# Mixer and norm order changed, x tiles loaded earlier: a two-pass decoder layer on Trainium2

## The chip, the cores and the metric

The kernel runs on the 8 cores of one Trainium2 chip. Each core does its own share of the tokens; nothing is exchanged between cores. The metric is the device time in microseconds of the slowest core, as the median of several runs. A change of more than 2% counts as faster or slower.

## What is computed

One decoder layer, cut to its core:

```python
h = x + 0.5 * rmsnorm(swiglu(rmsnorm(x, g1), wg1, wu1, wd1), p1)
n = rmsnorm(h, gm)
b_a, c_a, h_a, u, v = split(n @ w_in)
y_a = b_a * causal_dwconv3(c_a * h_a)
y_b = u * (tril(w_s[head]) @ rmsnorm(v) + b_s[head])
h = h + rmsnorm(concat(rmsnorm(y_a), rmsnorm(y_b)) @ w_out, pm)
h = h + 0.5 * rmsnorm(swiglu(rmsnorm(h, g2), wg2, wu2, wd2), p2)
h = h + rmsnorm(sigmoid(h @ w_pg) * (p @ w_pp), pp)
```

The model width is 1024, the hidden width 2816, and each core has 2048 prompt tokens (one sequence) and 128 sample tokens (16 sequences of 8).

## The kernel before

A core works its 17 blocks of 128 tokens in two passes: pass 0 has 9 blocks (8 of the prompt, 1 of samples) in three column tiles of 384, pass 1 has 8 blocks in two tiles of 512. Each pass goes through the same stages: gate and up products of the first FFN (`gu_stage`), its down product (`tok_stage`), the mixer, the output projection (`tok_stage`), the second FFN, and the per-layer embedding (`ple`). PE is busy nearly all the time.

Weights come in 44 "fills" a pass. A fill is two DMAs issued by POOL (L259, cast from f32 to bf16) into one of 8 slots of a ring. Before fill f, POOL waits until its slot is released by PE and fill f-3 has landed (`MAXFLY`, L255). `release` issues the next fill, or, where `hold_fills` has set a limit, notes it as owed; `pay_owed` raises the limit and issues what is owed. These limits act while the program is written: what reaches the chip is the order of POOL's instructions and the waits that stand before them.

The first norm works on the transposed input. `xt_load` (L361, on SP's queue) brings an x tile, `x_square` (L465) squares it on ACT, `x_stat` (L477) sums over the channels with 8 matmuls against a matrix of ones and forms 1/rms on ACT, and `x_apply` (L489) writes the 8 normed pieces to nT on DVE. Each following matmul of the tile waits for its own piece only. At the start SP issues x tile 0, and tiles 1 and 2 once fills 0 and 1 (their first halves) have landed; 90 matmuls on ones keep PE busy meanwhile. The units of a `gu_stage` have hooks that put the next tile's norm between them.

The mixer works tile by tile: v products, the norm of the tile before (`norm_tile`, L735: statistic of y_b on PE, then 8 multiplies on DVE), b products (DVE multiplies them in, ACT squares them into one of 4 buffers `sq`), the spatial mix on PE (L784), the statistic of y_a (L799, 4 matmuls in `stat`, L692), and the u products. The last tile's norm is the hook `tail`, behind the first block of the output projection.

`ple` goes over groups of three blocks: gate products into three PSUM pairs (L538), a sigmoid of each on ACT, the embedding product (L853) into the pair that the sigmoid has freed, the product of the two on DVE, the norm, the sum, and the store of y (L872, SP's queue). The result buffers `gb(b)` are six, so the sigmoid of block b waits for the store of block b-6 (`gb_guard`), and the first products of pass 1 write over buffers whose stores must have landed (`guard1`, L911). In pass 0, `ple` also starts the next pass: it loads both x tiles of pass 1 once the last transposed block has landed, squares tile 0 behind group 1, and does its statistic and its multiplies in group 2.

## Time and profile before

| | |
|---|---|
| median of 3 runs | 1377.72 us (1377.32 to 1531.78) |
| the profiled execution | 1379.56 us |
| its span, slowest core (7) | 1378.5 us |
| PE busy in the span | 1305.4 us (95%) |
| DVE, ACT busy | 524.1 us (38%), 415.0 us (30%) |

All times inside the execution are read from core 7, from the start of its span. "[idle before <-releaser]" at the end of a row is how long the engine had stood still before it, and what ended that.

### The profile page before, as it was taken

The numbers are of one execution on the slowest core, as the hardware profiler recorded it, in microseconds if no ns is written. First come the engines' busy times: TensorE is split into PE (matmuls) and PEld (weight loads), VectorE is DVE, ScalarE is ACT, GpSimd is POOL, SyncE is SP. The second block draws the span as 40 slices with busy tenths as digits, with TensorE's granted clock in tenths as the row PEclk, the third lists the DMA queues.
The fourth block names the chain that finished last, engine by engine and source line by source line (L and its number), as shares of the span: only waits on it lengthen the run. The fifth ranks groups of instructions, "written<-read, shape, count | busy, mean of one in ns | idle before, by whom it ended". The sixth has DMA issues, their size and how long they took to land.

```text
span 1378.5 us, 18493 instructions; the slowest of 8 cores (1363.9 to 1378.5 us)
## 1 busy us (share of the span) xinstructions
PE 1305.4 (95%) x6710; PEld 647.0 (47%) x6710; DVE 524.1 (38%) x691; ACT 415.0 (30%) x860; POOL 94.3 (7%) x185
## 2 busy tenths in 40 slices
PE   5999999999989999999996999999999899999995
PEld 3566664455445666644441444444444344444442
DVE  2322223356677222213365322223466922221337
ACT  3311112344355111111175111123333721111136
POOL 2100000001000200000010000000010020000000
PEclk8999999999999999999997999999999999999998
DMA  9997422129525963231289974321295297423123
GB/s 215 178 222 154 68 47 46 31 45 183 92 42 82 175 124 62 47 69 25 45 202 211 220 159 87 63 53 31 62 175 107 50 147 141 91 48 68 31 39 122
DMA packets 88185, 139.87 MB, mean 101 GB/s; under 512 B 58272, under 2 KB 58528, under 8 KB 87456
## 3 DMA queue, kind: packets, MB, share of 16 engines
q0 software_dynamic: 25296, 90.25, 39.7%
q1 hardware_dynamic: 62800, 48.43, 13.2%
q8 instruction: 56, 0.92, 0.3%
q14 instruction: 33, 0.27, 0.1%
HBM read 206.03 MB, written 9.51 MB: 156 GB/s over the span
## 4 chain that ended last, share of the span: by engine, by line
PE 84%; DVE 6%; DMA 3%; issue 3%; ACT 3%; POOL 0%; DVEq 0%; ACTq 0%; POOLq 0%; SPq 0%
PE ps L218 56%; PE ps L538 23%; PE ps L527 3%; DMA y<-big 2%; DVE zsc L227 2%; DVE nT L227 1%; DVE big L231 1%; DMA h<-xT 1%; ACT big L223 1%; DVE big L227 1%; DMA ring<-w 1%; ACT nT L223 1%; ACT sg L223 1%; ACT L223 1%; DVE nbr L227 1%
## 5 line engine op out<-in xcount | busy, mean ns | idle before, releaser
L218 PE MATMUL ps<-nT,ring 128*128 128x384 bf16 (+1 forms) x4160 | 785.3, 351 | 18.7 <-DVE nT L227 9.2
L218 PEld LDWEIGHTS ps<-nT,ring 128*128 128x128 bf16 x4160 | 409.7, 99 | 392.3 <-issue 44.0
L231 DVE TENSOR_TENSOR big<-ps,sg 128x384 bf16<-128x384 f32 (+1 forms) x220 | 133.9, 610 | 489.4 <-PE ps L218 479.4
L538 PE MATMUL ps<-ring,big 128*128 128x512 bf16 x1320 | 285.5, 379 | 4.5 <-DVE big L231 4.5
L223 ACT ACTIVATE sg<-ps 128x384 f32<-128x384 f32 (+1 forms) x237 | 127.1, 537 | 506.4 <-PE ps L218 496.8
L538 PEld LDWEIGHTS ps<-ring,big 128*128 128x128 bf16 x1320 | 128.9, 98 | 161.0 <-issue 6.2
L259 POOL DMA_DIRECT2D ring<-w x170 | 89.9, 535 | 1104.5 <-PE ps L218 621.6
L223 ACT ACTIVATE big<-ps 128x1024 bf16<-128x1024 f32 (+4 forms) x88 | 75.4, 870 | 229.4 <-PE ps L538 192.4
L227 DVE SCALAR_TENSOR_TENSOR zsc<-ps,st,gains 128x1024 f32<-128x1024 f32 x51 | 65.4, 1282 | 192.5 <-ACT st L223 192.2
L538 PE MATMUL ps<-ring,nT 128*128 128x512 bf16 x480 | 105.4, 379 | 1.0 <-DVE big L231 1.0
L231 DVE TENSOR_TENSOR big<-ps,big 128x384 f32<-128x384 f32 (+3 forms) x77 | 50.8, 686 | 62.1 <-PE ps L218 34.4
L538 PEld LDWEIGHTS ps<-ring,nT 128*128 128x128 bf16 x480 | 46.6, 98 | 58.3 <-issue 3.0
L231 DVE TENSOR_TENSOR h<-h,zsc 128x1024 f32<-128x1024 f32 x51 | 62.5, 1225 | 5.3
L227 DVE SCALAR_TENSOR_TENSOR nbr<-h,st,gains 128x1024 bf16<-128x1024 f32 x34 | 43.6, 1282 | 36.6 <-ACT st L223 36.6
L223 ACT ACTIVATE nbr<-h 128x1024 bf16<-128x1024 f32 x34 | 35.9, 1057 | 59.6 <-DVE h L231 51.7
L223 ACT ACTIVATE st<-st 128x1 f32<-128x1 f32 x204 | 41.4, 203 | 18.5 <-ACT st L223 0.5
L223 ACT ACT_TABLE_LOAD x27 | 34.6, 1283 | 22.0 <-PE ps L218 9.0
L527 PE MATMUL ps<-ring,big 128*128 128x512 bf16 x176 | 38.6, 379 | 0.0
L223 ACT ACTIVATE big<-big 128x384 bf16<-128x384 f32 (+1 forms) x40 | 21.9, 566 | 44.1 <-DVE big L231 44.1
L218 PE MATMUL ps<-ring,nT 128*128 128x512 bf16 x136 | 30.2, 379 | 0.0
L853 PE MATMUL ps<-ring,big 128*128 128x512 bf16 x68 | 18.7, 421 | 9.2 <-ACT big L223 9.2
L527 PEld LDWEIGHTS ps<-ring,big 128*128 128x128 bf16 x176 | 17.2, 98 | 20.8
(63 smaller groups left out, 369.3 us busy)
## 6 DMA issues: line engine op xcount, KB each, us to landing
ring<-w POOLq DMA_DIRECT2D x170, 512.0 KB, 14.5
h<-x SPq DMA_DIRECT2D x17, 512.0 KB, 30.7
y<-big SPq DMA_DIRECT2D x13, 512.0 KB, 10.7
gains<-gain SPq DMA_DIRECT2D x12, 512.0 KB, 9.3
h<-xT SPq DMA_DIRECT2D x3, 1536.0 KB, 13.2
big<-xT SPq DMA_DIRECT2D x2, 2048.0 KB, 20.0
y<-zsc SPq DMA_DIRECT2D x4, 512.0 KB, 12.0
big<-pT POOLq DMA_DIRECT2D x2, 512.0 KB, 7.9
```

Source lines behind the costliest of these rows:

```text
L218: ins = nc.tensor.matmul(out_ap, l, r, start=(i == 0), stop=(i == n - 1))
L223: return ACT.mark(nc.scalar.activation(**kw))
L227: return DVE.mark(nc.vector.scalar_tensor_tensor(out=out, in0=in0, scalar=scalar, in1=in1, op0=op0, op1=op1))
L231: return DVE.mark(nc.vector.tensor_tensor(out=out, in0=in0, in1=in1, op=op))
L259: nc.gpsimd.dma_start(out=ring_t[:, s, o:o + HALF], in_=w_d[f % NFILL, :, o:o + HALF])))
L527: ins = nc.tensor.matmul(o.t, lhs(k), sv[:, k % per, half * 512:half * 512 + 512], start=(k == 0), stop=(k == nk - 1))
L538: ins = nc.tensor.matmul(o.t, lhs(k), sv, start=(k == 0), stop=(k == nk - 1))
L853: ins = nc.tensor.matmul(o.t, pT_v[:, k, b * 128:(b + 1) * 128], sv, start=(k == 0), stop=(k == 1))
```

## The change

At the start, x tile 1 is issued on SP right behind tile 0, tile 2 once POOL has issued two fills; 110 matmuls on ones; both tiles' statistics, then 40 more matmuls on ones, stand before the first product; tile 2 is squared and summed later, in two hooks. In the mixer, `norm_tile` is cut in two: the statistic stays behind the v products, the 8 multiplies go behind the spatial mix; the statistic of y_a goes behind the second u product; `sq` has 6 buffers. In `ple` of pass 0, x tile 0 of pass 1 is issued behind the last down product (hook `next_x`; the junk of `post_stat` is moved out of its place), is squared behind the second sigmoid into a region of its own, summed at the end of the embedding products of group 0, and applied in group 1; x tile 1 is issued behind the stores of group 0; `pay_owed` is called for one fill a group. The norm of tile 1 is cut in two hooks, 32 products later. In the last group of the last pass both embedding products go ahead of the gates, with a fourth pair. The diff, cut:

```diff
+    xt_load(PASSES[0], 1)
...
+    for _ in range(2):
+        issue_next()
     ev_pc = pchain(nc.gpsimd.memset(carry_t[:], 0.0))
+    xt_load(PASSES[0], 2, [ev_pc])
     while wr["issued"] < NSLOT:
         issue_next()
-    for ti in range(1, 3):
-        xt_load(PASSES[0], ti, [fill_ev[ti - 1][0]])
 
     act([ev_ones], out=st_t[:, 0, 0:1], in_=ones_t[:, 0:1], func=AF.Ln)
-    warm = banks[7]
-    PE.wait(ev_ones)
-    for _ in range(90):
-        ins = nc.tensor.matmul(warm.t[:, 0:128], ones_t[:], ones_t[:], start=True, stop=True)
-    warm.free = PE.mark(ins)
+
+    def warm_up(n):
+        PE.wait(ev_ones, banks[7].free)
+        for _ in range(n):
+            ins = nc.tensor.matmul(banks[7].t[:, 0:128], ones_t[:], ones_t[:], start=True, stop=True)
+        banks[7].free = PE.mark(ins)
+
+    warm_up(110)
...
+    def x_sq_at(P, ti):
+        c0, w = P.tiles[ti]
+        if (P.idx, ti) == (1, 0):
+            return bigf[:, 4096:6144].bitcast(BF16).rearrange("p (k s) -> p k s", k=8)
+        return nT_t[:, :, c0:c0 + w]
...
+        sqt = x_sq_at(P, ti)
         X = XT[P.idx, ti].rearrange("p (k s) -> p k s", k=8)
         sq = []
         for i in range(0, 8, 2):
-            o = nT_t[:, i:i + 2, c0:c0 + w]
+            o = sqt[:, i:i + 2, :]
...
-    def x_apply(P, ti, bank, e2):
+    def x_apply(P, ti, bank, e2, wait=None):
         c0, w = P.tiles[ti]
         X = XT[P.idx, ti].rearrange("p (k s) -> p k s", k=8)
         out = []
+        DVE.wait(wait)
...
-                hooks[b]()
+                hooks[b](ev)
...
-        sq = [bigf[:, ZR + 2048 + 256 * i:ZR + 2304 + 256 * i].bitcast(BF16) for i in range(4)]
+        sq = [bigf[:, o:o + 256].bitcast(BF16) for o in [ZR + 2048 + 256 * i for i in range(4)] + [ZR + 4096, ZR + 4352]]
...
-        def norm_tile(ti, bank_of=get_bank):
+        def norm_stat(ti, bank_of=get_bank):
+            c0, w = P.tiles[ti]
+            par = ti % 2
+            return rstd_bc(*stat(y_ev[ti][1], w, bank_of), zsc_t[:, par, 512:1024], w, rs_free[par])
+
+        def norm_apply(ti, e_b):
             c0, w = P.tiles[ti]
             par = ti % 2
             ra, rb = zsc_t[:, par, 0:512], zsc_t[:, par, 512:1024]
-            ya, yb, ev_u = y_ev[ti]
-            e_b = rstd_bc(*stat(yb, w, bank_of), rb, w, rs_free[par])
+            ya, _, ev_u = y_ev[ti]
...
-                norm_tile(ti - 1)
+                e_b = norm_stat(ti - 1)
...
-            e_a = rstd_bc(*stat(sqa, w), zsc_t[:, ti % 2, 0:512], w, rs_free[ti % 2])
+            if ti >= 1:
+                norm_apply(ti - 1, e_b)
             sqb = []
             for c in range(4):
                 b, evl = proj(fU, evU, ti, c)
+                if c == 1:
+                    e_a = rstd_bc(*stat(sqa, w), zsc_t[:, ti % 2, 0:512], w, rs_free[ti % 2])
...
-        def tail():
-            norm_tile(nt - 1, get_tp)
+        def tail(ev):
+            norm_apply(nt - 1, norm_stat(nt - 1, get_tp))
...
-            xt_load(N, 0, [nT_ev[P.nb - 1]])
-            xt_load(N, 1)
-            pay_owed([nT_ev[P.nb - 1]], NFILL + 3)
+            pay_owed([nT_ev[P.nb - 1]], NFILL + 1)
+        def embed(b, last, npair=3):
+            pair = get_pair(npair)
+            pt, lo, hi = pair
+            PE.wait(evp, pT_ev)
+            ins = None
+            for o, half in ((lo, 0), (hi, 1)):
+                for k in range(2):
+                    sv = ring_t[:, fp % NSLOT, k * 1024 + half * 512:k * 1024 + half * 512 + 512]
+                    ins = nc.tensor.matmul(o.t, pT_v[:, k, b * 128:(b + 1) * 128], sv, start=(k == 0), stop=(k == 1))
+            ev = PE.mark(ins)
+            if last:
+                release(fp, ev)
+            return pair, ev
...
+            early = N is None and lastg
+            if early:
+                emb = {b: embed(b, b == grp[-1], 4) for b in grp}
...
-                if N is not None and gi == 2 and b == grp[0]:
-                    xs["st"] = x_stat(N, 0, xs["sq"], get_tp)
...
+                if N is not None and b == 1:
+                    xs["sq"] = x_square(N, 0)
...
-                xs["sq"] = x_square(N, 0, [gate_ev[3]])
+                x_apply(N, 0, *xs["st"], [gate_ev[3]])
...
-            if N is not None and gi == 2:
-                xs["ev"] = x_apply(N, 0, *xs["st"])
+            if N is not None and gi == 0:
+                xs["st"] = x_stat(N, 0, xs["sq"], get_tp)
...
+            if N is not None and not lastg:
+                pay_owed(None, NFILL + 2 + gi)
+                if gi == 0:
+                    xt_load(N, 1, [xstat_ev[1, 0]])
...
-    x_apply(PASSES[0], 0, *x_stat(PASSES[0], 0, x_square(PASSES[0], 0), get_bank))
-
-    def start_mid(ti):
-        def f():
-            x_apply(PASSES[0], ti, *x_stat(PASSES[0], ti, x_square(PASSES[0], ti), get_bank))
-        return f
+    first = x_stat(PASSES[0], 0, x_square(PASSES[0], 0), get_bank)
+    x_apply(PASSES[0], 0, *first)
+    second = x_stat(PASSES[0], 1, x_square(PASSES[0], 1), get_bank)
+    warm_up(40)
+    x_apply(PASSES[0], 1, *second)
+
+    nx = {}
+
+    def start_square():
+        nx["sq"] = x_square(PASSES[0], 2)
+
+    def start_mid():
+        x_apply(PASSES[0], 2, *x_stat(PASSES[0], 2, nx["sq"], get_bank))
...
+    def next_square():
+        nx["sq"] = x_square(PASSES[1], 1)
+
     def next_mid():
-        e = x_apply(PASSES[1], 1, *x_stat(PASSES[1], 1, x_square(PASSES[1], 1), get_bank))
+        e = x_apply(PASSES[1], 1, *x_stat(PASSES[1], 1, nx["sq"], get_bank))
...
-            gu_stage(P, 2, guard1, {(0, 0): (0, start_mid(1)), (1, 0): (1, start_mid(2)), (2, 0): (0, start_loads),
+            gu_stage(P, 2, guard1, {(1, 0): (1, start_square), (1, 1): (0, start_mid), (2, 0): (0, start_loads),
...
-            gu_stage(P, 3, guard1, {(0, 0): (1, next_mid)})
+            gu_stage(P, 3, guard1, {(0, 0): (1, next_square), (1, 0): (1, next_mid)})
...
+        def next_x(ev):
+            xt_load(PASSES[1], 0, [ev])
...
-                  base + G2POST, 4.0, 1, 14, cast)
+                  base + G2POST, 4.0, 1, 0, cast, {8: next_x} if N is not None else None)
```

The order of DVE's instructions in the mixer of pass 0, from the last v multiply of the third tile to its last u multiply. `big<-ps,sv` is a v multiply, `nT<-big,gc,zsc` the multiplies of a tile's norm, `big<-ps,big` the b or u multiplies, `big<-ps,gc,bbc` the mix. Before:

```order
L231 TENSOR_TENSOR big<-ps,sv 128x512 x3
L231 TENSOR_TENSOR big<-big 128x512
L227 SCALAR_TENSOR_TENSOR nT<-big,gc,zsc 128x384 x8
L231 TENSOR_TENSOR big<-ps,big 128x384 x4
L227 SCALAR_TENSOR_TENSOR big<-ps,gc,bbc 128x256
...
L231 TENSOR_TENSOR big<-ps,big 128x384 x4
L227 SCALAR_TENSOR_TENSOR nT<-big,gc,zsc 128x384 x8
```

Now:

```order
L231 TENSOR_TENSOR big<-ps,sv 128x512 x3
L231 TENSOR_TENSOR big<-big 128x512
L231 TENSOR_TENSOR big<-ps,big 128x384 x4
L227 SCALAR_TENSOR_TENSOR big<-ps,gc,bbc 128x256
...
L227 SCALAR_TENSOR_TENSOR nT<-big,gc,zsc 128x384 x8
L231 TENSOR_TENSOR big<-ps,big 128x384 x4
L227 SCALAR_TENSOR_TENSOR nT<-big,gc,zsc 128x384 x8
```

The 8 multiplies of the second tile's norm have moved from ahead of the b multiplies to ahead of the u multiplies.

The order of ACT in `ple` of pass 0, group 0 and the start of group 1. `big<-ps 128x1024` is a sigmoid, `sg,st<-big` the sum of squares of a block, `ps<-ps 128x512 x2` the 1/rms of the x tile. Before:

```order
L223 ACTIVATE big<-ps 128x1024 x3
L223 ACTIVATE sg,st<-big 128x1024
L223 ACTIVATE st<-st 128x1 x2
...
L223 ACTIVATE big<-ps 128x1024
L223 ACTIVATE zsc<-ps 128x1024 x2
L223 ACTIVATE nT<-big 128x2x512 x4
```

Now:

```order
L223 ACTIVATE big<-ps 128x1024 x2
L223 ACTIVATE big<-big 128x1024 x4
L223 ACTIVATE big<-ps 128x1024
L223 ACTIVATE sg,st<-big 128x1024
L223 ACTIVATE st<-st 128x1 x2
...
L223 ACTIVATE ps<-ps 128x512 x2
L223 ACTIVATE big<-ps 128x1024
L223 ACTIVATE zsc<-ps 128x1024 x2
```

The four squares of the x tile stood behind the sigmoids of group 1 and stand now between the second and the third sigmoid of group 0.

The order of SP's queue at the same place. Before:

```order
L325 DMA_TRANSPOSE nT<-nbr 128x8x128 [waits sem_dve,t1]
L293 DMA gains<-gain 128x1024
L361 DMA big<-xT 128x4096 [waits t0]
L361 DMA big<-xT 128x4096
L872 DMA y<-big 128x1024 [waits sem_dve] x4
L872 DMA y<-zsc 128x1024 [waits sem_dve] x2
```

Now:

```order
L361 DMA big<-xT 128x4096 [waits sem_pe]
L325 DMA_TRANSPOSE nT<-nbr 128x8x128 [waits sem_dve,t1]
L293 DMA gains<-gain 128x1024
L901 DMA y<-big 128x1024 [waits sem_dve] x3
L361 DMA big<-xT 128x4096 [waits sem_pe]
L901 DMA y<-big 128x1024 [waits sem_dve]
L901 DMA y<-zsc 128x1024 [waits sem_dve] x2
```

The first x tile has gone ahead of the last transpose, the second behind three stores. POOL's rows for the fills of this place now (t0 is the last transposed block, xt1 the second x tile, slotN_M the landing of a half fill); they are the same, with the same waits, before:

```order
L259 DMA ring<-w 128x2048 [waits t0,sem_pe,slot1_0,slot1_1]
L259 DMA ring<-w 128x2048
L259 DMA ring<-w 128x2048 [waits sem_pe,slot2_0,slot2_1]
L259 DMA ring<-w 128x2048
L259 DMA ring<-w 128x2048 [waits sem_pe,slot3_0]
L259 DMA ring<-w 128x2048
L259 DMA ring<-w 128x2048 [waits xt1,sem_pe,slot4_0,slot4_1]
```

Here nothing has moved.

## Rows read from the trace of the kernel before

**Rows 1.** The cores: span and mean granted clock.

```profile
core 0: 1363.9 us, clock 0.981
core 7: 1378.5 us, clock 0.976
```

**Rows 2.** Two of PE's waits, core 7: us in total, times, longest.

```profile
PE ps L692 <- ACT big L223: 10.3, 11, 3.5
PE ps L853 <- ACT big L223: 9.2, 4, 3.4
```

**Rows 3.** Timeline of the start: start us, us, engine, line, operation, count, idle before.

```profile
1.41 7.52 PE L393 MATMUL ps<-ones 128*128 128x128 bf16 x90 [1.41 <-POOL ones L371]
...
9.96 1.58 ACT L223 ACTIVATE nT<-h 128x768 bf16<-128x768 f32 x2 [7.12 <-DMA h<-xT]
...
27.19 3.04 ACT L223 ACTIVATE nT<-h 128x768 bf16<-128x768 f32 x4 [6.59 <-DMA h<-xT]
28.18 3.00 PE L484 MATMUL ps<-nT,ones 128*128 128x384 bf16 x8 [7.46 <-ACT nT L223]
...
57.40 149.82 PE L218 MATMUL ps<-nT,ring 128*128 128x384 bf16 x921 [0.20 <-DVE nT L227]
```

**Rows 4.** DMA queue of SP, 18 to 26 us: packets, MB, share of 16 engines.

```profile
q1 hardware_dynamic: 133, 1.56, 55.0%
```

**Rows 5.** Timeline of the mixer of pass 0, third tile.

```profile
378.07 4.31 DVE L227 SCALAR_TENSOR_TENSOR nT<-big,gc,zsc 128x384 bf16<-128x384 f32 x8
...
383.61 1.72 PE L692 MATMUL ps<-big,ones 128*128 128x384 bf16 x4 [3.46 <-ACT big L223]
384.17 2.68 DVE L227 SCALAR_TENSOR_TENSOR big<-ps,gc,bbc 128x256 f32<-128x256 f32 x8
385.17 7.04 PE L218 MATMUL ps<-nT,ring 128*128 128x384 bf16 x32
...
393.23 3.61 PE L538 MATMUL ps<-ring,nT 128*128 128x512 bf16 x16 [1.02 <-DVE big L231]
```

**Rows 6.** Timeline of the mixer of pass 1, second tile.

```profile
1052.63 0.38 PE L692 MATMUL ps<-big,ones 128*128 128x512 bf16 x1 [2.77 <-ACT big L223]
...
1054.81 8.48 PE L218 MATMUL ps<-nT,ring 128*128 128x512 bf16 x32
```

**Rows 7.** Timeline from `ple` of pass 0 into pass 1, core 7.

```profile
694.47 0.80 SPq L361 DMA_DIRECT2D big<-xT  x2
...
710.26 3.88 ACT L223 ACTIVATE nT<-big 128x1024 bf16<-128x1024 f32 x4
...
724.93 1.28 ACT L223 ACT_TABLE_LOAD   x1 [3.46 <-DMA y<-big]
...
727.39 1.86 PE L853 MATMUL ps<-ring,big 128*128 128x512 bf16 x4 [3.38 <-ACT big L223]
...
740.30 11.20 PE L218 MATMUL ps<-nT,ring 128*128 128x512 bf16 x32 [2.20 <-DVE nT L227]
...
758.16 0.69 DVE L231 TENSOR_TENSOR big<-ps,sg 128x512 bf16<-128x512 f32 x1 [5.83 <-DMA y<-big]
...
769.72 5.52 PE L218 MATMUL ps<-nT,ring 128*128 128x512 bf16 x17 [2.65 <-DVE nT L227]
```

**Rows 8.** DMA queues on core 7, 694 to 702 us, then 722 to 746 us.

```profile
q1 hardware_dynamic: 208, 1.57, 82.0%
q0 software_dynamic: 2, 0.01, 0.7%
...
q0 software_dynamic: 731, 2.67, 73.6%
q1 hardware_dynamic: 732, 2.67, 29.4%
```

**Rows 9.** Timeline of core 0 at the same place as rows 7.

```profile
758.03 17.21 PE L218 MATMUL ps<-nT,ring 128*128 128x512 bf16 x77 [0.33 <-DVE nT L227]
```

**Rows 10.** Timeline of the end, DVE.

```profile
1366.16 2.35 DVE L231 TENSOR_TENSOR big<-ps,big 128x1024 f32<-128x1024 f32 x2
```

32 lines of the change are left out of this document (13 added, 19 removed).

## The prediction

> **What bounds the kernel now.** I read the span of each core first, then PE's waits, then the timeline around each wait. The slowest core is 7 with 1378.5 us, the fastest core 0 with 1363.9 [rows 1]; the profiled execution took 1379.56, so 1.1 lies outside the span, and it is 1.8 above the median of 1377.72. PE is busy 95% of the span: the floor is its matmuls, which the change leaves alone, and what can be won is where PE stands still or runs at the lower clock. PE's waits name the places: for the squares of the mixer 10.3 us, for sigmoids 9.2 [rows 2], and for the squares of one x tile 7.46 at once [rows 3]. Their neighbours matter too, since the clock falls behind an idle stretch: 32 matmuls of the mixer take 7.04 us behind a wait of 3.46 [rows 5], where 32 at the pace of 921 in 149.82 us [rows 3], 0.163 each, take 5.2.
>
> **The start.** Before, the stream without gaps begins at 57.4 us. The order has 1056 products in this stage, 921 of them are in that row, so 135 are done by then [rows 3]. Now the first product waits for the statistic of tile 1. Tile 0 lands at 9.96 as before (its squares start there). Tile 1 is behind it on the same queue, which moved 1.56 MB, one tile, in 8 us while fills shared the engines [rows 4]: it lands at about 17.3, where before its squares began at 27.19. Four squares take 3.04, and the matmuls that follow them one by one ended at 31.2, 4.0 behind the first square [rows 3]; so the statistic is done at 21.2. The 40 matmuls on ones cost 3.3 us at the pace of the first 90 (7.52 us) and 6.7 at half the clock; PE has idled since 12.5, so I take 5, and the first product starts at 26. 112 products at 0.163 bring 44.3. The squares of tile 2 are put only 16 products ahead of its statistic, the statistic ends at 46.9, a table load and two functions later (2.5) DVE begins the 8 pieces, which at 0.54 each (4.31 for 8 [rows 5]) hold PE until 54.0 with the 136th product. Before, that one started at 57.4 too: **-3.5 us**. If tile 1 landed only at 27.2 as before, it is +6; if it landed alone, at 14, and the clock held, it is -8. DMA is not the limit behind it: the first fill is needed at 26, the second some 10 us later.
>
> **The mixer.** Removed in pass 0: waits for the squares of y_a of 3.46 in the third tile [rows 5], and 2.0 and 0.3 in the other two; the pace of the four statistic matmuls, 1.72 instead of 0.65 [rows 5], three times (3.2); the lower clock behind two of the waits, 1.8 each [rows 5]. That is 12.6. Given back: DVE now does the 8 multiplies (4.31) between the mix (2.68) and the u multiplies (about 2). From the end of its v multiplies it has b 2 + 2.7 + 4.3 + 2 = 11 us of work, PE 11.9 for the same stretch; but DVE starts its mix only when PE has finished it, and is then 9 us from the end, PE 6. The squares queue later on ACT too, so the third tile's v norm runs some 2 us late. The output projection starts in the PSUM pair of the last u product: I expect a wait of 5.6 instead of 1.02 [rows 5], 4.6 more, and a lower clock behind it, about 2.5. Net **-5.5**. Pass 1: 2.77 and 0.4 of waits, pace 2.6 (four statistic matmuls from 1052.63 to 1054.81 where 0.216 each is 0.9, two tiles), clock 1.5 (8.48, and 32 at 0.216 are 6.9) [rows 6] come to 7.3; the pair that the projection takes is there that of the second u product, so the new wait is about 1.8: **-5.5**. Both between 0 (DVE becomes the bound) and the whole 12.6 and 7.3. The two more `sq` buffers only carry this order.
>
> **From `ple` into pass 1.** Before, x tiles 0 and 1 are issued together at 694.5 [rows 7], and the stores of y stand behind them. The first store has landed at 724.9, and the table load and sigmoid of block 6 waited for it; PE waited 3.38 [rows 7], and 8.5 in the three waits of this group (9.2 less 0.7 at the end of the kernel) [rows 2]. Then 2.2 before the first product, embedding products at the lower clock (1.86, about 0.85 each too much, three), 32 products in 11.2 where 0.216 each (3.61 for 16 [rows 5]) gives 7, and 2.65 at 769.7 [rows 7]. Now tile 0 is issued at 685.9, behind the last down product, 8.6 earlier. It is 2.1 MB; at 1.57 MB from 694.5 to 702 [rows 8] it takes 9 and lands near 697. But ACT does its squares, 3.88 [rows 7], before the third sigmoid: that one ends near 702, and the third embedding product, due at 698, waits 4.1 and costs 1.7 of clock. So: 740.3 less 8.5, 2.2 and 2.5 is 727.1; plus 4.1, 1.7 and 1.5 (the multiply that frees the last pair) is 734.4 for the first product of pass 1. The stores 0 to 2 are issued near 708, 710 and 713 with no x tile ahead of them and take 4.7 each (2.67 MB in 24 us beside fills [rows 8]): 715, 720, 725, and their sigmoids want them at 721, 725 and 729. Then 96 products, 8 of the statistic and 8 more at 0.216 end at 758.6; before, that was 769.72 + 3.5 = 773.2 [rows 7].
> The new late thing is DVE: the multiplies of tile 1 stand behind four products whose places wait for stores 6 to 8 (5.83 idle for one of them before [rows 7]). x tile 1 sits behind stores 0 to 2 and lands near 736, stores 3 to 5 behind it. POOL's next fill waits for x tile 1 too, and its bytes come late: of the fills issued behind the x tiles of 694.47, 2 packets had moved by 702 [rows 7, 8]. I take 4 to 5 us in which SP's queue has the engines alone, and a store takes 1.4 (29.4% of 24 us for 2.67 MB [rows 8]). Stores 3 to 5 are through at 741, 6 to 8 at 4.7 each at 742, 747 and 751.5, DVE begins tile 1's multiplies at 753.4 and ends them at 758: PE loses 1.4 to their pace. End 760: **-13**. On core 0 the stage was 11.7 earlier [rows 9] and I expect 6 to 8. From below: no gain at all (next part); from above 17, if the tile lands before 694 and ACT never holds PE.
> How SP's and POOL's queues share: from 722 to 746 us they moved 732 and 731 packets, 2.67 MB each, while fills took 73.6% and stores 29.4% of the engines' time [rows 8]. They alternate packet by packet, so the cheap packets go at the pace of the dear ones.
> The Trainium skill says the same (DMA: Bandwidth & Descriptors, section "Queues, rings and completion order": each engine goes round its queues a packet at a time); were time shared evenly instead, a store would take 2.8 and not 4.7, the multiplies would never be late, and the sum would be 1.4 lower.
>
> **The rest.** "One fill per group" does nothing on the chip: POOL's rows there are the same as before, with the same waits, so all three fills go out at once, now about 3 us later, since the last transpose is behind the x tile. 0, the first is needed at 734. The early embedding products in the last group: DVE is the bound there, its two products start at 1366.16 behind the sums of group 1 [rows 10]; the gates end some 2 to 3 us later, about when DVE gets to them. 0, between -1 and +2. The moved junk and the junk's place: same instruction, 0.
> **Sum:** 1379.6 - 3.5 - 5.5 - 5.5 - 13 = 1352.1. Against the median, which is 1.8 lower, it would be a little less, against the risk that another core is now the slowest a little more: **1352**.
>
> **The rivals.**
> A, the stores drain no faster (0.20): fills never leave the engines free, stores 3 to 8 take 4.7 each from 736 to 764, the multiplies of tile 1 begin near 766, PE waits for them and for the places of the first products, and the stage ends at 773 as before. For it: fills had 73.6% of the engines' time through this stretch [rows 8], and x tile 1 is now behind three stores. Against: the fill behind xt1. 1352.1 + 13 = 1365.
> B, the waits really go (0.23): x tile 1 at the start lands near 14, x tile 0 of pass 1 before 694 as on cores with faster memory, the lower clock does not come. 1352.1 - 3 - 4 - 3 = 1342.
> C, the stores become the bound (0.04): the same place as A, with the stores later than before. Each us by which store 8 lands after 764 is a us of PE. The rest of the change is worth 14.5, so it decides from a landing at 779 on, for instance if SP's queue moves x tile 1 at half the pace of rows 4. At 784 it is 1384, slower than before.
> D, the fills are paced after all (0.03): stores then run at 1.4 each, 1350.
> The forecast itself has 0.50.
>
> **How the numbers follow.** The forecast's own spread, from the bounds of start and mixer, is 1343 to 1360. 2% of the median is 27.6, about what a measurement of this kernel can tell from no change, so faster begins below 1350.2: a third of the forecast's half, nearly all of B and half of D, 0.42. Slower is C, 0.04. Within: 0.54. A range of 1339 to 1367 takes in A and most of B, and leaves out C and the low end of B.
>
> **What would show it.** Tile 1's squares at 17 us and the stream without gaps from 54; no wait of PE at the y_a statistic, a wait of 5 before the output projection; sigmoids 6 to 8 not held by a store; PE's wait at the third embedding product; the first product of pass 1 some 6 us sooner than before, counted from the last down product, and the first product of its tile 1 some 13; the cores closer together than 14.6. Wrong would be: PE waiting at the fourth product of pass 1 for a store (A), or no wait at the third embedding product (B).

## The result and the profile after

The changed kernel takes 1371.7 us in the median of 4 runs (1356.94 to 1444.76) against 1389.78 for the kernel before (1377.32 to 1531.78); the ratio is 0.986, with a 95% interval of 0.981 to 0.991. That is a gain of 1.4%, within 2%: the same by that bound, and smaller than forecast. The profiled execution took 1360.08 us where that of before took 1379.56: 19.5 us less, and 27.5 were forecast.

Both medians hold two executions in which some cores ran at a lower granted clock (0.81) for 160 us or more, which happens whatever the kernel; without these the changed kernel took 1356.94 and 1360.08 us and the one before 1377.32 and 1377.72, the ratio above and all whole times below are of executions without such cores, and a "mean of cores" is over all cores that were free of it, also where no whole execution was. The forecast was 1352 with a range of 1339 to 1367: 1358.5, the middle of the two, lies inside it, and the median of 1371.7 outside.

The cores of the changed kernel in the profiled execution, which answer to [rows 1]:

```profile
core 2: 1359.0 us, clock 0.980
...
core 6: 1357.8 us, clock 0.983
core 7: 1348.8 us, clock 0.985
```

The forecast's core, 7, went from 1378.5 to 1348.8, 29.7 us less, and another core, 2, is now the slowest (it had 1374.0). Which core is slow changes from one execution of a kernel to the next (core 7 of the changed kernel had 1354.4 in the execution of 1356.94), so a single core compared with itself says little: slowest against slowest it is 19.5 us less, and the mean of the eight cores went from 1371.5 to 1352.9, 18.6 less.

PE's waits on core 2, for [rows 2] (us in total, times, longest):

```profile
PE ps L553 <- DVE big L231: 10.0, 6, 4.3
PE ps L218 <- DVE zsc L227: 9.1, 3, 7.0
...
PE ps L218 <- DVE big L231: 5.6, 2, 5.4
...
PE ps L858 <- ACT big L223: 3.4, 1, 3.4
```

The 10.3 us for the statistic of y_a are gone, and the waits of the embedding products for ScalarE's sigmoids fell from 9.2 to 3.4. (The 7.0 us for `zsc` stand before the second FFN of pass 1 and were there before.) New are 4.3 us for DVE before the output projection, which was forecast as 5.6, and 5.4 us for DVE before the first product of pass 1, which was forecast as 1.5.

The start (PE's timeline on core 2: start, us, engine, line, operation, count, idle before), for [rows 3]:

```profile
19.67 3.00 PE L498 MATMUL ps<-nT,ones 128*128 128x384 bf16 x8 [7.18 <-ACT nT L223]
22.46 3.63 PE L396 MATMUL ps<-ones 128*128 128x128 bf16 x40
25.93 18.36 PE L218 MATMUL ps<-nT,ring 128*128 128x384 bf16 x112
44.13 1.46 PE L498 MATMUL ps<-nT,ones 128*128 128x384 bf16 x8
...
52.55 22.69 PE L218 MATMUL ps<-nT,ring 128*128 128x384 bf16 x129 [0.20 <-DVE nT L227]
```

The 136th product starts at 52.55 instead of 57.40 and 54.0 forecast. Behind it the granted clock was 0.53 from 52.5 to 56.0 us: 129 products take 22.69 us, where the pace of [rows 3] gives 21.0. The third tile of the mixer of pass 0, for [rows 5], PE first, then DVE:

```profile
373.32 0.81 PE L707 MATMUL ps<-big,ones 128*128 128x384 bf16 x4
373.97 2.76 PE L218 MATMUL ps<-nT,ring 128*128 128x384 bf16 x16
381.02 6.48 PE L553 MATMUL ps<-ring,nT 128*128 128x512 bf16 x16 [4.29 <-DVE big L231]
```

```profile
374.48 4.31 DVE L227 SCALAR_TENSOR_TENSOR nT<-big,gc,zsc 128x384 bf16<-128x384 f32 x8
378.71 1.94 DVE L231 TENSOR_TENSOR big<-ps,big 128x384 f32<-128x384 f32 x4
```

No wait at the statistic (L707) any more; but the four multiplies that empty the u products' banks (L231) start only when the eight norm multiplies are through, PE waits 4.29 us, and the next 16 matmuls take 6.48 us where [rows 5] has 3.61: the granted clock was 0.51 from 380 to 387 us, its lower level.

From the gates into pass 1, for [rows 7], core 2, PE and then DVE:

```profile
676.34 10.52 PE L553 MATMUL ps<-ring,nT 128*128 128x512 bf16 x48
...
691.97 1.87 PE L858 MATMUL ps<-ring,big 128*128 128x512 bf16 x4 [3.38 <-ACT big L223]
...
728.80 15.34 PE L218 MATMUL ps<-nT,ring 128*128 128x512 bf16 x64 [5.38 <-DVE big L231]
```

```profile
712.22 5.35 DVE L227 SCALAR_TENSOR_TENSOR nT<-big,gc,ps 128x512 bf16<-128x512 f32 x8
717.49 1.28 DVE L227 SCALAR_TENSOR_TENSOR big<-big,st,gains 128x1024 f32<-128x1024 f32 x1
...
725.06 3.48 DVE L231 TENSOR_TENSOR big<-ps,big 128x1024 f32<-128x1024 f32 x3
...
732.02 1.28 DVE L227 SCALAR_TENSOR_TENSOR big<-big,st,gains 128x1024 f32<-128x1024 f32 x1
...
743.45 0.69 DVE L231 TENSOR_TENSOR big<-ps,sg 128x512 bf16<-128x512 f32 x1 [6.29 <-DMA y<-big]
748.22 1.29 DVE L231 TENSOR_TENSOR big<-ps,sg 128x512 bf16<-128x512 f32 x2 [4.08 <-DMA y<-big]
752.08 0.69 DVE L231 TENSOR_TENSOR big<-ps,sg 128x512 bf16<-128x512 f32 x1 [2.57 <-DMA y<-big]
752.69 5.35 DVE L227 SCALAR_TENSOR_TENSOR nT<-big,gc,ps 128x512 bf16<-128x512 f32 x8
```

These rows hold the answer of the study. DVE works from 712 to 737 with one gap of 0.95 us (at 728.5): the x tile's eight multiplies, six instructions of group 1's norms, the three products of group 2 (which free PE's pairs), six of its norms. Then it stands still for three stores of y, and the multiplies of x tile 1 are queued behind. So 5.38 us of PE (on all eight cores: 5.38 or 5.39) are DVE's queue, and the rest is when the last group's stores have landed. The lower clock follows here too: the 64 products behind the wait take 15.34 us on core 2 and 16.76 on core 7, where 0.216 each makes 13.8.

Where the time went, as means over the eight cores of each profiled execution (read from each core's timeline; us):

| stretch | before | changed |
|---|---|---|
| span's start to pass 0's output projection | 393.0 | 380.5 |
| from there to the gates of pass 0 | 292.4 | 294.4 |
| gates to pass 1's first product | 50.2 | 49.6 |
| from there to pass 1's output projection | 320.5 | 312.7 |
| from there to the end | 315.4 | 315.7 |

The second row is the lower clock behind the 4.29 us wait, which falls into the projection. The third shows the miss: 0.6 us in the mean.

### The profile page after: what moved, and what is told of

The parts are those of the page before. It is cut to its first block, busy times and chain, and to the rows that moved or that the text cites. A ratio compares the mean times of both kernels' runs of the same rounds, so it can differ in the third digit from the quotient of the medians.

```text
span 1359.0 us, 18605 instructions; the slowest of 8 cores (1348.5 to 1359.0 us)
## 1 busy us (share of the span) xinstructions
PE 1300.9 (96%) x6770; PEld 650.7 (48%) x6770; DVE 523.6 (39%) x691; ACT 410.3 (30%) x858; POOL 94.3 (7%) x185
## 4 chain that ended last, share of the span: by engine, by line
PE 84%; DVE 6%; DMA 4%; issue 3%; ACT 2%; DVEq 0%; SPq 0%; ACTq 0%
PE ps L218 55%; PE ps L553 24%; PE ps L542 3%; DVE nT L227 2%; DVE zsc L227 2%; DMA h<-xT 1%; DVE big L231 1%; DMA y<-big 1%; DVE big L227 1%; DMA big<-xT 1%; ACT sg L223 1%; PE ps L498 1%; DVE nbr L227 1%; ACT big L223 1%; ACT L223 0%
## 5 line engine op out<-in xcount | busy, mean ns | idle before, releaser
L231 DVE TENSOR_TENSOR big<-ps,sg 128x384 bf16<-128x384 f32 (+1 forms) x220 | 134.1, 611 | 495.2 <-PE ps L218 476.0
L553 PE MATMUL ps<-ring,big 128*128 128x512 bf16 x1320 | 285.5, 379 | 4.4 <-DVE big L231 4.4
L553 PE MATMUL ps<-ring,nT 128*128 128x512 bf16 x480 | 108.3, 386 | 5.7 <-DVE big L231 5.7
L231 DVE TENSOR_TENSOR big<-ps,big 128x384 f32<-128x384 f32 (+3 forms) x77 | 50.1, 686 | 46.3 <-PE ps L858 22.7
L231 DVE TENSOR_TENSOR h<-h,zsc 128x1024 f32<-128x1024 f32 x51 | 62.5, 1226 | 5.7 <-DVE zsc L227 0.5
L223 ACT ACTIVATE st<-st 128x1 f32<-128x1 f32 x204 | 41.4, 203 | 18.2 <-ACT st L223 0.4
L542 PE MATMUL ps<-ring,big 128*128 128x512 bf16 x176 | 38.6, 379 | 0.0
L223 ACT ACTIVATE big<-big 128x384 bf16<-128x384 f32 (+2 forms) x44 | 25.0, 604 | 39.6 <-DVE big L231 37.1
L218 PE MATMUL ps<-ring,nT 128*128 128x512 bf16 x136 | 30.2, 379 | 0.0
L227 DVE SCALAR_TENSOR_TENSOR nT<-big,gc,zsc 128x384 bf16<-128x384 f32 (+1 forms) x40 | 23.9, 666 | 9.0 <-ACT zsc L223 9.0
## 6 DMA issues: line engine op xcount, KB each, us to landing
big<-xT SPq DMA_DIRECT2D x2, 2048.0 KB, 14.7
```

Source lines behind the costliest of these rows:

```text
L218: ins = nc.tensor.matmul(out_ap, l, r, start=(i == 0), stop=(i == n - 1))
L223: return ACT.mark(nc.scalar.activation(**kw))
L227: return DVE.mark(nc.vector.scalar_tensor_tensor(out=out, in0=in0, scalar=scalar, in1=in1, op0=op0, op1=op1))
L231: return DVE.mark(nc.vector.tensor_tensor(out=out, in0=in0, in1=in1, op=op))
L542: ins = nc.tensor.matmul(o.t, lhs(k), sv[:, k % per, half * 512:half * 512 + 512], start=(k == 0), stop=(k == nk - 1))
L553: ins = nc.tensor.matmul(o.t, lhs(k), sv, start=(k == 0), stop=(k == nk - 1))
```

## The experiments

The columns of the tables are the times of whole executions (the slowest core), the ratio to the kernel before with its 95% interval, and the mean of cores: 1371.4 us for the kernel before from 220 cores, 1353.2 for the changed kernel from 116. This mean repeats within 0.9 us (the kernel before, measured five times, had 1371.0 to 1371.9; the changed kernel, three times, 1352.9 to 1353.4), so a difference of 1 us between two versions is not shown to be a gain or a loss.

### One part of the change at a time

Each of the three kernels has one part of the change and the old code for the rest; what they change is the part of the diff shown ahead of the prediction. First the start alone:

```diff
+    xt_load(PASSES[0], 1)
...
+    xt_load(PASSES[0], 2, [ev_pc])
...
-    for ti in range(1, 3):
-        xt_load(PASSES[0], ti, [fill_ev[ti - 1][0]])
```

> Only the start is changed (tile order, warm-up, hooks). Theory 1 (the parts add up as the two traces show, about 3.3 us here): the 136th product starts near 52.5 instead of 57.4 us, the mixer of pass 0 some 4 us sooner, every later stage as long as before, time 3 to 5 us (0.3%) below the kernel before. Theory 2 (the earlier stream meets something later, a fill or a clock step, that gives it back): the mixer starts 4 us sooner but the time is the same within 1 us.

The mixer alone:

```diff
-            if ti >= 1:
-                norm_tile(ti - 1)
+            if ti >= 1:
+                e_b = norm_stat(ti - 1)
...
+            if ti >= 1:
+                norm_apply(ti - 1, e_b)
```

> Only the mixer's order is changed. Theory 1 (parts add up): no wait of PE at the statistic of y_a, a wait of 4 to 5 us before the output projection of pass 0 and 1 to 2 in pass 1; 6 us gained in pass 0 and 5 in pass 1, time 11 us (0.8%) below the kernel before. Rival (DVE's later norm moves the whole gain to the projection): at most 4 us.

`ple` alone, with the x tile behind the last down product, its squares, statistic and multiplies earlier, tile 1's norm in two hooks and the early embedding products:

```diff
-            xt_load(N, 0, [nT_ev[P.nb - 1]])
-            xt_load(N, 1)
...
+                if N is not None and b == 1:
+                    xs["sq"] = x_square(N, 0)
...
+            if N is not None and gi == 1:
+                x_apply(N, 0, *xs["st"], [gate_ev[3]])
```

> Only the way from ple of pass 0 into pass 1 (with the early embedding products at the end) is changed. Theory 1 (DVE takes the place of the stores: the 8 multiplies of the x tile stand ahead of group 1's norm): PE waits 5.4 us for DVE before the first product of pass 1 on every core, the stage from ple to the mixer of pass 1 takes 284 to 291 us on all cores where it took 284 to 296, slowest core 5 us (0.35%) below the kernel before, fast cores unchanged. Rival (the forecast's sizes were right and only the choice of the core was wrong): 10 us or more on the slowest core.

| kernel | slowest core | ratio, interval | mean of cores |
|---|---|---|---|
| head_only | 1372.6 to 1373.9 | 0.997 (0.996 to 0.999) | 1366.5 |
| mixer_only | 1365.6 to 1367.8 | 0.992 (0.991 to 0.994) | 1360.6 |
| ple_only | 1369.8 to 1371.2 | 0.995 (0.993 to 0.998) | 1366.8 |

By the ratios the start is worth 3.9 us and the mixer 10.7, as forecast (3.5, and 5.5 twice). `ple` is worth 6.6 (4.6 in the mean of the cores) and not 13, and in its trace PE waits 5.3 to 5.4 us for DVE before pass 1 on every core: Theory 1 in all three. The product of the three ratios is 0.985 and the whole kernel has 0.986, so the parts add up within the intervals; in the mean of cores they sum to 20.3 us (4.9, 10.8, 4.6) where the whole has 18.2. Of the 8 us that the profiled execution lacks to the forecast, 6.4 are the third part's.

### Which half of the mixer part earns

The norm multiplies stay where the change puts them, but the statistic of y_a is back ahead of the u products, with four buffers for squares (cut):

```diff
+            e_a = rstd_bc(*stat(sqa, w), zsc_t[:, ti % 2, 0:512], w, rs_free[ti % 2])
             sqb = []
             for c in range(4):
                 b, evl = proj(fU, evU, ti, c)
-                if c == 1:
-                    e_a = rstd_bc(*stat(sqa, w), zsc_t[:, ti % 2, 0:512], w, rs_free[ti % 2])
```

> Changed kernel with the mixer part cut in two: the norm multiplies stay behind the mixing products, but the statistic of the first half is back ahead of the u products, and the squares have four buffers again and not six. Theory A (the mixer's gain is the wait of that statistic for ScalarE's squares, which the u products now cover): 1.5 to 3 us per tile-stage come back, 6 to 9 us in all, ratio to the changed kernel 1.005 to 1.007. Theory B (the gain is the order of the norm multiplies alone): within 2 us of the changed kernel.

One whole execution took 1359.2 us, the mean of 34 cores is 1354.2: 1 us above the changed kernel, so theory B. On core 3 the statistic of the third tile has no wait, though it stands in its old place, and over the whole kernel 1.7 us of such waits are left of the 10.3:

```profile
373.14 1.59 PE L707 MATMUL ps<-big,ones 128*128 128x384 bf16 x4
374.57 5.36 PE L218 MATMUL ps<-nT,ring 128*128 128x384 bf16 x32
382.70 5.30 PE L553 MATMUL ps<-ring,nT 128*128 128x512 bf16 x16 [2.77 <-DVE big L231]
```

The wait of 3.46 us in [rows 5] was named after ScalarE's squares, but these waited for DVE's y multiplies, which stood behind the eight norm multiplies. Taking those eight out of the way was enough; the later statistic and the two buffers are worth 1 us together at most, which is no more than the mean of cores repeats by.

### The new wait before the output projection

```diff
-            if ti >= 1:
+            late = P.idx == 0 and ti == nt - 1
+            if ti >= 1 and not late:
                 norm_apply(ti - 1, e_b)
...
+            if late:
+                norm_apply(ti - 1, e_b)
```

> The changed kernel as it is, beside the three below on one chip, so that they can be compared with it and not only with the kernel before. Expected by every theory: ratio to the kernel before 0.985 to 0.987, the first product of pass 1 waiting 5.4 us for VectorE on every core.

> Changed kernel, but in the last tile of pass 0's mixer the eight norm multiplies of the tile before stand on VectorE behind the four multiplies that empty the u products' banks, and no longer ahead of them. Theory A (the 4.3 us wait before pass 0's output projection is VectorE's queue: eight multiplies of some 0.45 to 0.5 us lie ahead of the multiply that frees the pair, and TensorE comes back at the low clock): the wait falls to under 1 us, the next row runs at the high clock, the stage shortens by 4 to 6 us; ratio to the changed kernel 0.996. Theory B (the eight multiplies are only paid later, in the projection's own post-norm): the output projection stalls at its fourth block, which reads what they write, and the gain is under 1.5 us, ratio 0.999 to 1.000.

changed_again: 1357.3 to 1358.8 us, mean of 44 cores 1353.4. outproj_first: 1352.45 to 1354.02, mean of 40 cores 1347.8, 5.6 below it: theory A. On core 1 of outproj_first:

```profile
374.72 2.76 PE L218 MATMUL ps<-nT,ring 128*128 128x384 bf16 x16
378.50 3.61 PE L553 MATMUL ps<-ring,nT 128*128 128x512 bf16 x16 [1.02 <-DVE big L231]
```

The wait is the 1.02 us of [rows 5] again, the next row runs at 3.61, and DVE's 16 multiplies in a row hold nobody up.

### VectorE's queue ahead of pass 1

Two edits. In apply_first the x tile's multiplies stand ahead of group 1's products instead of behind them, at a place where DVE stood still for 6 us:

```diff
+            if N is not None and gi == 1:
+                x_apply(N, 0, *xs["st"], [gate_ev[3]])
             zev = {}
...
-            if N is not None and gi == 1:
-                x_apply(N, 0, *xs["st"], [gate_ev[3]])
```

> The changed kernel, with the 8 multiplies of the next x tile put ahead of the products of group 1 in DVE's queue, where DVE was idle for 6.0 us. Theory 1 (DVE's queue sets the start of pass 1): the wait before the first product of pass 1 falls from 5.4 to about 1.5 us, stores 3 to 8 go out about 5 us sooner, and the time is 3 to 4 us below the changed kernel (ratio to before about 0.983). Rival (the stores and x tile 1 set it): the first product comes 4 us sooner, but the wait for the multiplies of tile 1, 0.8 us, grows by as much and the time is that of the changed kernel.

In squares_b2 the squares of the x tile are behind the third sigmoid:

```diff
-                if N is not None and b == 1:
+                if N is not None and b == 2:
                     xs["sq"] = x_square(N, 0)
```

> Changed kernel with the four squares of pass 1's first x tile issued on ScalarE behind the third sigmoid of the first gate group and not behind the second. Theory A (the 3.4 us wait of the third embedding product, and the low clock behind it, are ScalarE's: it stands at the squares until the x tile has landed, with the third sigmoid queued behind): that wait falls to under 1 us, and the stretch from the gates to pass 1 shortens by 3 to 5 us; ratio to the changed kernel 0.997. Theory B (the time only moves: the squares end 5 us later, the statistic and so the multiplies are late, and VectorE's queue frees the last pair as late as before): the wait before pass 1 grows by about what the embedding gains, ratio 0.999 to 1.001.

> Changed kernel with three edits together: the x tile's multiplies ahead of group 1's products (as apply_first), the squares behind the third sigmoid (as squares_b2), and the norm multiplies behind the u multiplies in pass 0's last mixer tile (as outproj_first). If each is worth what theory A of it says, 3 + 4 + 5 = 12 us below the changed kernel, some 1348 us, ratio to the kernel before 0.977. If the waits only move, within 2 us of the changed kernel.

apply_first: 1356.0 to 1357.2 us, ratio 0.985 (0.983 to 0.987), mean of 44 cores 1352.2, 1.0 below the changed kernel: the rival, not Theory 1 with its 3 to 4 us. The wait before pass 1 fell to 2.19 on all cores; core 5:

```profile
724.74 15.66 PE L218 MATMUL ps<-nT,ring 128*128 128x512 bf16 x64 [2.19 <-DVE big L231]
```

So 3.2 us are gone there, the stretch before pass 1 is 47.2 us instead of 49.6, and yet 1 us at most comes out at the end: the next stretch grew from 312.7 to 314.0. Half of the gain moved into pass 1.

squares_b2 has a mean of cores alone: 1352.5 from 18 cores, 0.7 below the changed kernel, so theory B for the time. The wait of the third embedding product is gone, and gates to pass 1 take 47.5 us on every core, 47.6 at most, where the changed kernel has 47.7 to 52.5: ScalarE, standing at the squares until the x tile has landed, was what made the cores differ in this stretch. Again it comes back: on the two cores of the trace that can be read here (6 and 7), pass 1's first product to the output projection takes 314.8 and 313.5.

three_together: one whole execution with 1352.54 us, mean of 48 cores 1349.6, which is 1.8 above outproj_first alone. Both theories fell. With the late squares, the statistic is late too, and the multiplies put ahead of group 1's products hold those back (core 0: the gates of group 2 wait 3.71 us for DVE); the stretch is 50.4 us. The two edits exclude each other. Without apply_first:

> Changed kernel with the squares behind the third sigmoid and the norm multiplies behind the u multiplies in pass 0's last mixer tile; the x tile's multiplies stand where the change puts them (behind group 1's products). Theory A (the two gains stand in different stages and add: 5 us in front of the output projection, 1.8 us in the mean and up to 5 us on the cores with a late x tile at the third embedding product): 5 to 8 us below the changed kernel, about 1350 us, ratio to the kernel before 0.980 to 0.982, and the stretch from the gates to pass 1 47.5 us on all cores. Theory B (what three_together showed, the stretch at 50 us, comes from the late squares by themselves): the stretch stays at 50 us and the time at that of outproj_first.

two_together has a mean of cores alone: 1346.9 from 30 cores, none above 1350.2 (1353.0 in outproj_first). The stretch before pass 1 is 47.5 us on all eight, as theory A has it. The time is 6.3 us below the changed kernel, inside theory A's 5 to 8, but only 0.9 below outproj_first, which is theory B's time: the next stretch grew from 312.3 us there to 314.1. So the late squares even out the cores and add at most 1 us in the mean.

### What ends the stretch: the queue, or the stores behind it

The same with group 1's norms put behind group 2's products:

```diff
-            st = {}
+            if gi != 2 or N is None:
+                st = {}
...
+            if N is not None and gi == 1:
+                pay_owed(None, NFILL + 3)
+                continue
-            for b in grp:
+            for b in (groups[1] + grp if N is not None and gi == 2 else grp):
```

> As two_together, but with the three norms of gate group 1 (six VectorE instructions, 3 x 1.3 + 3 x 0.7 us or so) behind the three products of group 2, so that only the eight multiplies of the x tile are left ahead of the products that free the last pairs. Theory A (the 5.4 us before pass 1 is the length of VectorE's queue): the wait falls to under 2.5 us and pass 1's first product comes 3 us sooner after the gates; but the stores of group 1 leave 5 us later, and the multiplies of x tile 1 that wait for stores give 2 us or more of it back: ratio to two_together 0.998 to 1.001. Theory B (it is the depth of the chain embedding, product, bank and not the queue): the wait stays above 5 us.

The wait before pass 1 is 2.19 us or less and the first product comes 3 us sooner, as theory A has it. But the kernel is 10 us slower than two_together (one whole execution, 1361.67; mean of 32 cores 1357.0), far outside what I gave. On core 3, DVE then PE:

```profile
729.02 1.23 DVE L231 TENSOR_TENSOR big<-big,h 128x1024 f32<-128x1024 f32 x1
744.81 0.69 DVE L231 TENSOR_TENSOR big<-ps,sg 128x512 bf16<-128x512 f32 x1 [14.57 <-DMA y<-big]
```

```profile
745.76 9.14 PE L218 MATMUL ps<-nT,ring 128*128 128x512 bf16 x32 [14.70 <-DVE big L231]
```

The same row on core 3 of two_together:

```profile
733.21 0.69 DVE L231 TENSOR_TENSOR big<-ps,sg 128x512 bf16<-128x512 f32 x1 [6.54 <-DMA y<-big]
```

PE's eight banks no longer cover it. The hidden columns that pass 1 writes first lie where `gb` keeps blocks 6, 7 and 8 (`guard1`), so its first multiply waits for the last group's store. DVE being late with that group's sums is only a third of it. Counted from the last down product, block 6's sum ends at 54.2 to 55.0 us, where two_together has 50.9, but DVE goes on at 68.9 to 74.5 instead of 60.9 to 62.4: the store needs 14.7 to 19.6 us from its sum and not 10.0 to 11.5. SP issues group 1's three stores right ahead of it, between 46.7 and 52.5 us instead of 38.9 and 44. So the backlog of stores counts as well as the time at which DVE lets them go; no run takes the two apart. Rival to both: that the fills running beside the stores make them slow.

```diff
-                pay_owed(None, NFILL + 2 + gi)
+                pay_owed([e], NFILL + 2 + gi)
```

> Changed kernel, but the fills of groups 0 and 1 really paced: each waits on GpSimd for the last add of its group, at some 705 and 722 us instead of 688. Theory A (all three fills at once cost the second x tile and the stores their bandwidth, and so the waits of 6.3, 4.1 and 2.6 us of VectorE for stores after pass 1's start): these waits get shorter, x tile 1 lands sooner, and the time falls by 1 to 2 us. Theory B (the waits are for when the stores are issued, which VectorE's own queue sets): the same time within 1 us, ratio to the changed kernel 0.9993 to 1.0007, and the three waits within 0.5 us of what they were.

1357.3 to 1358.2 us, ratio 0.986 (0.983 to 0.989), mean of 40 cores 1352.4, 0.8 below the changed kernel. DVE's three waits there are 5.0, 4.0 and 3.7 us in the mean of the eight cores, against 5.6, 4.1 and 3.2 in changed_again, the same in sum: theory B. It moves the fills (GpSimd's rows are at 687, 702 and 721 us on core 2 instead of one at 689), but not the end.

Then the buffers themselves, turned by three, so that pass 1's first hidden columns lie where group 1's blocks were, stored long before:

```diff
-        i = b % 6
+        i = (b + 3) % 6
...
-        return [guards["zsc"] if b % 6 >= 4 else None, out_ev.get(b - 6) if b >= 6 else None]
+        return [guards["zsc"] if (b + 3) % 6 >= 4 else None, out_ev.get(b - 6) if b >= 6 else None]
...
-            evs = [out_ev.get(x + 6 if x < 3 else x) for x in range(lo, hi + 1) if x < 4]
+            evs = [out_ev.get(x + 3) for x in range(lo, hi + 1) if x < 4]
...
-        zfree[0], zfree[1] = out_ev[4], out_ev[5]
+        zfree[0], zfree[1] = out_ev[7], out_ev[8 if P.nb == 9 else 2]
```

> Changed kernel with the six buffers of the gates' blocks turned by three: groups 0 and 2 have big's fourth part and the two of zsc, group 1 big's first three, which pass 1's first hidden columns overwrite. Theory A (the rest of the forecast went into the wait of VectorE's first products of pass 1 for stores of the last group): the waits of 6.4, 3.9 and 2.6 us for y stores are gone, the stretch from pass 1's first product to its output projection falls from 312.9 us to 309 to 311, ratio to the changed kernel 0.9980 to 0.9990. Theory B (TensorE's eight banks cover these waits, and the multiplies of x tile 1 and the clock set the stretch): the store waits go, the stretch stays at 312 to 313 us and the time within 1 us.

> two_together with the buffers turned. Theory A: the stretch from pass 1's first product to its output projection falls from 314.1 us to 310 to 311, with 47.5 us before it as there: 3 to 4 us below two_together, slowest core at 1346 to 1347 us. Theory B: 314 us as there.

> norms_late with the buffers turned: all of group 1's norms are behind group 2's products, so group 1's stores leave late as well. Theory A (the 14.6 and 9.6 us of VectorE for a store in norms_late were for the last group's store, behind six norms): the wait falls to under 5 us, the stretch from 327.1 to some 314 to 317 us, 10 to 13 us below norms_late, and near two_together in all. Theory B (it was the queue of norms on VectorE itself, 12 instructions ahead of pass 1's first multiply): the stretch stays above 322 us.

| kernel | slowest core | ratio, interval | mean of cores | gates to pass 1 | then to output projection |
|---|---|---|---|---|---|
| changed kernel | 1356.9 to 1360.2 | 0.986 (0.981 to 0.991) | 1353.2 | 49.6 | 312.7 |
| slots_turned | 1352.5 to 1354.0 | 0.982 (0.980 to 0.985) | 1349.2 | 49.6 | 308.9 |
| two_together | none | | 1346.9 | 47.5 | 314.1 |
| slots_two | 1345.0, 1345.5 | 0.977 (0.972 to 0.981) | 1342.5 | 47.5 | 308.7 |
| norms_late | 1361.7 | | 1357.0 | 44.6 | 327.1 |
| slots_late | 1348.3 to 1348.8 | 0.979 (0.975 to 0.983) | 1342.4 | 44.3 | 312.1 |

Theory A in all three, and a little beyond its range each time (slots_late gains 14.6 us on norms_late where 10 to 13 were given). On core 2 of slots_two the wait for a store is gone, and x tile 1's multiplies start behind their own statistic:

```profile
725.90 1.23 DVE L231 TENSOR_TENSOR zsc<-zsc,h 128x1024 f32<-128x1024 f32 x1
727.04 0.68 DVE L231 TENSOR_TENSOR big<-ps,sg 128x512 bf16<-128x512 f32 x1
...
739.52 5.36 DVE L227 SCALAR_TENSOR_TENSOR nT<-big,gc,ps 128x512 bf16<-128x512 f32 x8 [3.59 <-ACT ps L223]
```

```profile
718.76 16.30 PE L218 MATMUL ps<-nT,ring 128*128 128x512 bf16 x64 [4.25 <-DVE zsc L231]
734.90 1.89 PE L498 MATMUL ps<-nT,ones 128*128 128x512 bf16 x8
736.62 33.62 PE L218 MATMUL ps<-nT,ring 128*128 128x512 bf16 x155
```

PE runs from 718.8 to 874 without a gap. With the buffers in the old place the late squares gave 2.1 us before pass 1 and lost 1.4 behind it; here they keep them. slots_late is even with it in the mean, but its slowest core is 3 us behind slots_two: group 1's stores are late there, and now hold the buffers (on core 6 DVE waits 4.42 us for one).

### The end, and the best version again

late_embedding takes the early embedding products of the last group out:

```diff
-            early = N is None and lastg
+            early = False
```

> The changed kernel again, as the measure for the two beside it. By every theory 1357 to 1359 us, ratio to the kernel before 0.986.

> Changed kernel without its early embedding products: in the last group of pass 1 they stand behind the gates again, in three pairs. Theory A (VectorE is the bound there, it reaches these products only behind the sums of the group before): the time from the output projection of pass 1's mixer to the end is within 0.7 us of the changed kernel's, ratio to it 0.9995 to 1.0005. Theory B (the early products let VectorE start sooner, or hold the gates up): 1 to 3 us to one side or the other.

> slots_two once more, beside the changed kernel. Theory A (what the three edits take away are waits that stand on every core): 1345 to 1346 us again, ratio to the changed kernel 0.990 to 0.992 and to the kernel before 0.976 to 0.978, the cores within 5 us of each other. Rival (the first result was a good chip): over 1350 us.

changed_third: 1357.5 to 1360.2 us. late_embedding: 1357.0 to 1360.5, ratio to before 0.986 (0.984 to 0.988), and from the gates of pass 1 to the end 48.9 to 49.0 us in both, on every core. Theory A: worth nothing. slots_two_again has a mean of cores alone, 1342.6 from 40 cores, the highest 1344.8 (slots_two: 1342.5 and 1344.4), against 1353.2 and 1359.2 for changed_third beside it. So the mean core's gain of some 11 us over the changed kernel was measured twice; the time of a whole execution rests on the two of slots_two.

## Why the prediction was wrong

**The start: right in size, by two errors that cancel.** Forecast -3.5. The statistic of tile 2 ended at 45.6 and not 46.9 us, so the gapless stream begins at 52.55 us, 4.85 earlier than before. But behind the piecewise start the clock was at its lower level (0.53 from 52.5 to 56.0 us), which the sum did not have: the 921 products take 151.39 us instead of 149.82, and the mixer begins at 290.4 instead of 293.7: -3.3. head_only gives -3.9.

**The mixer: right in size, one reason wrong.** Forecast -5.5 and -5.5; from the mixer's start to the gates the two profiled cores differ by 6.05, in pass 1 by 5.1, and mixer_only gives 10.7 for both. The new wait was 4.3 and not 5.6, with the lower clock behind it as forecast. What was wrong is whose wait it was: the sum booked it as a wait for ScalarE's squares and took the six buffers as needed for the new order, and norms_alone shows that the place of the norm multiplies earns all but 1 us.

**`ple` into pass 1: the step that failed.** Forecast: -13 on core 7, -6 to -8 on core 0, so that the slowest core gains 13. On core 7 the stretch went from 296.0 to 283.7 us, -12.3. But core 0 went from 283.7 to 284.8, the mean from 289.5 to 286.5, and core 2, now the slowest, has 290.9. Longest against longest that is 5.1 us less and not 13, mean 3.0, shortest 0. What the change was to take away did go: the sigmoids of blocks 6 to 8 no longer wait for a store. Two terms of the sum were mis-sized, and both stand on DVE:

- "1.5 (the multiply that frees the last pair)" is 5.38 us on every core. I placed the x tile's eight multiplies behind group 1's products and did not carry them on to group 2's products, 5.35 and 7.6 us of norms later. On core 7 the wait for ScalarE was 1.96 and not 4.1, with no lower clock behind it, so the first product came 48.3 us after the last down product where I had 48.5: two errors that cancelled. On core 2 ScalarE's wait (3.38) and the lower clock came about as forecast, nothing cancelled, and it is 52.5.
- "Stores 6 to 8 at 4.7 each at 742, 747 and 751.5" counted the queue and not the engine that issues the stores. That is 56, 61 and 66 us behind the last down product. On core 2 DVE could go on at 67.1, 71.9 and 75.7. Block 6 is summed only at 732.1, at the end of the run of DVE work above; no queue could have had its store through by 732. Nor was 4.7 its price: from the end of its sum to DVE going on it took 9.2 to 12.0 us on the 24 cores of the changed kernel's three traces. Tile 1's multiplies, which I had begin at 753.4 (67.5), began at 76.3 on core 2 and 71.2 on core 7.

A third term was left at nothing: the lower clock behind the wait before pass 1, 1.5 us on core 2 and 2.9 on core 7.

The rest of the miss is that I made the sum on the slowest core of before. Core 7 was slow since its x tile and stores were late, and the change takes that away: but what then ends the stretch, DVE's queue and the stores it issues, stands on every core. A fast core had nothing to gain and got eight multiplies more in that queue: gates to pass 1 took 45.4 to 54.6 us before and takes 47.7 to 52.5 now.

**The rivals.** A (stores drain no faster, the stretch ends as before) is nearest for the mean core, though by another mechanism: not the fills beside the stores, which fills_paced shows to be without effect, but the time at which DVE's sums let the stores go and, as norms_late shows, the stores ahead of them in SP's queue. PE's wait at the fourth product of pass 1 did not come. B did not happen, and C did not either. D is excluded by fills_paced: paced fills are worth no more than the mean of cores repeats by. The Trainium skill's rule that an engine goes round its queues a packet at a time (DMA: Bandwidth & Descriptors, "Queues, rings and completion order") stood beside a difference of 1.4 us; no run here tells it apart.

**The rest: right.** The early embedding products are worth 0, and "one fill per group" did not pace: all three went out at 688.6 us, in six issues in a row.

What stays open is what sets when the x tile lands (ScalarE could start its squares 8.4 to 10.7 us behind the issue on the 24 cores of the changed kernel's traces), and so which cores are the slow ones in one execution; it differs between executions of the same kernel.

## What to carry to other kernels

When work is moved earlier, walk the queue of the engine that gets it to the end: here eight multiplies, well placed for what they feed, delayed the products that free PE's banks and the stores that free the next stage's buffers, and half or more of what was won ahead of a stage was lost behind it until the buffers themselves were turned (4 us for four changed lines). Before pricing a transfer by its queue's speed, look at when its issuer can issue it and at what stands ahead of it then. And price a change on a fast core as well as on the slowest: what evens the cores out gives the slowest one only the distance to the next bound.

## What the runs showed of the hardware

The lower clock (1.2 of 2.4 GHz) followed the waits of 4.3 to 4.7 us before the output projection on all 24 cores of the changed kernel's three traces: 16 matmuls took 4.9 to 6.6 us instead of 3.61, and with the wait at 1.02 or 1.24 it did not come on any of outproj_first's eight. At the third embedding product it stayed away after the waits of 2.04 us or less (12 cores). Of the 12 with 2.61 to 3.63 us, nine had it in the product's row or the next; three, with 2.87, 3.10 and 3.19, did not. So the length of one such wait does not settle it. Shortening such a wait can pay more than its length: outproj_first took 3.3 us of wait away and gained 5.6.

A store of 512 KB took 2.7 us from issue to landing in the median of fills_paced and 3.4 to 6.4 in the changed kernel's executions, but the one that DVE waits for took 9.2 to 12.0 (on core 2, block 6, summed at 732.1, through at 743.4), and 14.7 to 19.6 in norms_late, where three others go out right ahead of it. A median over a kernel's transfers is no price for the one on the path.
